# Two heads' attention scores issued together from the two halves of the TensorE array, in every second step of the attention loops

## What is computed

```python
# first block, one layer: heads of 64 columns (A: two maps of 32)
s = einsum('bqhmd,bkhmd->bhmqk', qa, ka_all) * 32 ** -0.5       # A: 4 heads, difference of two softmaxes
p = softmax(s);  a = p[:, :, 0] - lam * p[:, :, 1];  oa = einsum('bhqk,bkhd->bqhd', a, va_all)
s = einsum('bqhgd,bkhd->bhgqk', qb, kb_all) * 64 ** -0.5        # B: 6 heads, 2 key/value heads
s_nb, s_cx = ...                                                # C: 6 heads, neighbourhood with a bias, and context
# layer 0 also attends from the context tokens (to the context alone, 256 keys)

# second block, dilated attention: for each head and group g with (window, dilation)
scores = einsum(q_g, k_g) * 64 ** -0.5; scores = where(valid, scores, -inf)
o = sum_g alpha_g * softmax(scores_g) @ v_g                     # alpha from the groups' log-sums
```

## Time and profile before

| | |
|---|---|
| median of three runs | 1380.77 us (1374.21, 1380.77, 1384.84) |
| profiled execution, span from first to last instruction | 1381.9 us |
| mean granted TensorE clock | 0.954 of full |
| TensorE matmuls busy | 1213.9 us, 88% |
| TensorE weight loads busy | 958.0 us, 69% |
| VectorE busy | 756.3 us, 55% |
| ScalarE busy | 607.9 us, 44% |
| GpSimd busy | 253.1 us, 18% |
| DMA | 158.63 MB, 115 GB/s on the mean |

### The profile page before, as it was taken

How to read it: one execution, slowest core, us unless ns; L and a number is a source line. 1 busy time by engine, 2 the same in 40 slices (tenths; PEclk the granted TensorE clock), 3 DMA queues, 4 the chain that set the end, 5 groups by cost and what they waited for, 6 DMA issues and landing times.

```text
span 1381.9 us, 16760 instructions
## 1 busy us (share of the span) xinstructions
PE 1213.9 (88%) x5909; PEld 958.0 (69%) x5909; DVE 756.3 (55%) x1361; ACT 607.9 (44%) x1178; POOL 253.1 (18%) x323
## 2 busy tenths in 40 slices
PE   2678588889999797689999989898969999999997
PEld 2666356767666586567776768687858887888885
DVE  2746358478665264354445466665466555565533
ACT  2043244343665245345446454344344444444553
POOL 5108014024400312230230012100012211121100
PEclk9998789899999899889999999999989999999999
DMA  6518624333310322312220176454536665334301
GB/s 189 183 61 228 126 76 126 107 107 92 107 47 1 95 82 92 102 46 62 77 65 28 62 264 196 152 155 138 179 119 187 183 184 157 118 116 123 111 1 46
DMA packets 79475, 158.63 MB, mean 115 GB/s; under 512 B 5910, under 2 KB 6206, under 8 KB 79136
## 3 DMA queue, kind: packets, MB, share of 16 engines
q1 hardware_dynamic: 74992, 145.82, 34.5%
q0 software_dynamic: 4400, 11.73, 3.9%
HBM read 154.39 MB, written 3.78 MB: 114 GB/s over the span
## 4 chain that ended last, share of the span: by engine, by line
PE 69%; DVE 9%; ACT 8%; DMA 5%; POOL 4%; issue 4%; SPq 0%; ACTq 0%; POOLq 0%; DVEq 0%
PE bank L612 16%; PE bank L614 15%; PE bank L613 15%; PE bank L714 5%; PE bank L739 4%; DMA raw<-in_w_ada_dram 4%; PE bank L724 3%; PE bank L784 3%; PE bank L810 2%; DVE work L1486 2%; POOL small L1324 2%; DVE w_lo L1464 2%; ACT w_hi L906 2%; PE bank L795 2%; PE bank L632 1%
## 5 line engine op out<-in xcount | busy, mean ns | idle before, releaser
L612 PE MATMUL bank<-w_lo,h_hi 128*128 128x512 f32 (+1 forms) x1152 | 468.2, 406 | 48.5 <-DVE h_lo L1534 15.4
L614 PE MATMUL bank<-w_hi,h_hi 128*128 128x512 f32 (+1 forms) x1152 | 451.7, 392 | 0.0
L613 PE MATMUL bank<-w_hi,h_lo 128*128 128x512 f32 (+1 forms) x1152 | 451.5, 392 | 0.0
L1464 DVE TENSOR_TENSOR w_lo<-raw,w_hi 128x1024 fp32r<-128x1024 f32 x224 | 285.8, 1283 | 302.7 <-ACT w_hi L906 301.0
L906 ACT ACTIVATE w_hi<-raw 128x1024 fp32r<-128x1024 f32 x224 | 236.1, 1058 | 328.6 <-PE bank L614 268.8
L612 PEld LDWEIGHTS bank<-w_lo,h_hi 128*128 128x128 f32 x1152 | 225.9, 196 | 103.6 <-issue 32.7
L614 PEld LDWEIGHTS bank<-w_hi,h_hi 128*128 128x128 f32 x1152 | 224.5, 195 | 45.7
L613 PEld LDWEIGHTS bank<-w_hi,h_lo 128*128 128x128 f32 x1152 | 226.4, 197 | 41.0 <-issue 0.5
L1486 DVE SCALAR_TENSOR_TENSOR work<-raw,cvec,work 128x512 f32<-128x512 f32 x138 | 98.1, 764 | 34.2 <-DMA raw<-in_w_ada_dram 33.9
L714 PE MATMUL bank<-work 64*128 64x512 f32 (+3 forms) x240 | 99.6, 596 | 12.2 <-ACT stage L1082 12.2
L739 PE MATMUL bank<-work,stage 128*128 128x128 f32 x640 | 92.2, 286 | 1.8 <-ACT stage L1091 1.6
(11 more groups left out here) (161 smaller groups left out, 1167.0 us busy)
## 6 DMA issues: line engine op xcount, KB each, us to landing
raw<-in_b_w_in_dram SPq DMA_DIRECT2D x80, 512.0 KB, 3.7
raw<-in_w_in_dram SPq DMA_DIRECT2D x56, 512.0 KB, 3.8
raw<-in_w_ada_dram SPq DMA_DIRECT2D x48, 512.0 KB, 3.8
raw<-in_a_w_in_dram SPq DMA_DIRECT2D x48, 512.0 KB, 4.1
raw<-in_w_out_dram SPq DMA_DIRECT2D x16, 512.0 KB, 3.8
raw<-in_a_w_out_dram SPq DMA_DIRECT2D x16, 512.0 KB, 3.7
raw<-in_b_w_out_dram SPq DMA_DIRECT2D x8, 512.0 KB, 3.7
work<-bias POOLq DMA_DIRECT2D x24, 96.0 KB, 4.2
```

Source lines behind the costliest of these rows:

```text
L612: pe.matmul(bank, hT(h_hi, ph, kt, tt), w_lo[:, s, k, lo:lo + w], start=first, stop=False)
L613: pe.matmul(bank, hT(h_lo, ph, kt, tt), w_hi[:, s, k, lo:lo + w], start=False, stop=False)
L614: mm = pe.matmul(bank, hT(h_hi, ph, kt, tt), w_hi[:, s, k, lo:lo + w], start=False, stop=last)
L1464: dve.tensor_tensor(w_lo[:, i % SPLIT, :, :], raw[:, PIECE_AT[p] % RAW, :, :], w_hi[:, i % SPLIT, :, :].bitcast(F32), ALU.subtract).then_i ...
```

## The change

In every second step TensorE issues the scores of two units instead of one, and none in the other steps. The two units are heads in different halves of the array. For that B's heads are taken in the order 0, 3, 1, 4, 2, 5, and the dilated units in the order tile 0 of two heads, then tile 1 of the same two. A is scored one unit at a time as before. In the dilated attention the two units' matmuls alternate, group by group; its tile-1 units are paired only when four score banks are there. All other parts of a step keep their place, and go by the new order of units. The order of work on the other engines is changed by the order of units alone.

```diff
-    return [(layer, qt, kind, h) for kind, n in (("A", A_HEADS), ("B", B_HEADS), ("C", C_HEADS))
-            for qt in (ALL_TILES if layer == 0 else X_TILES) for h in range(n)]
+    return [(layer, qt, kind, h) for kind, order in (("A", range(A_HEADS)), ("B", (0, 3, 1, 4, 2, 5)), ("C", range(C_HEADS)))
+            for qt in (ALL_TILES if layer == 0 else X_TILES) for h in order]
+
+
+def scored_at(units, i):
+
+    if i + 1 >= len(units):
+        return ()
+    if units[i + 1][2] == "A":
+        return (i + 1,)
+    return (i + 1, i + 2) if i % 2 else ()
+
+
+def dil_unit(i):
+
+    return i % 4 // 2, i // 4 * 2 + i % 2
+
+
+def dil_scored_at(i, solo):
+
+    if i % 4 == 3:
+        return (i + 1, i + 2)
+    if i % 4 == 1:
+        return (i + 1, i + 2) if i > solo else (i + 1,)
+    return (i + 1,) if i % 4 == 2 and i - 1 <= solo else ()
...
-                    if i + 1 < len(units):
-                        score(units[i + 1], i)
+                    for n in scored_at(units, i):
+                        score(units[n], i)
...
-                units = [(qt, h) for h in range(DIL_HEADS) for qt in X_TILES]
+                units = [dil_unit(i) for i in range(2 * DIL_HEADS)]
...
-                def score(i):
-                    qt, h = units[i]
...
+                def score(*pair):
+                    for i in pair:
+                        qt, h = units[i]
...
+                        ring = SCORE_BANKS if i <= solo else SCORE_BANKS + (2, 3)
+                        for second in range(qt + 1):
+                            take(pe, ring[s_use[0] % len(ring)], "dscore", i, second)
+                            s_use[0] += 1
                     for g in range(DIL):
...
+                        for i in pair:
+                            qt, h = units[i]
+                            nk = (qt + 1) * P
+                            base = (h % 2) * HD
+                            at, second = dil_score_place(i, g)
+                            mm = pe.matmul(bank_of("dscore", i, second)[:, at:at + nk], dqkT[base:base + HD, g * 16 + h // 2, qt * P:(qt + 1) * P],
+                                           dqkT[base:base + HD, g * 16 + 8 + h // 2, 0:nk], start=True, stop=True)
+                            if g == DIL - 1:
+                                mm.then_inc(*scores.at(("dil", i)))
...
                     if i == 0:
-                        score(0)
-                    if i + 1 < len(units):
-                        score(i + 1)
+                        score(0, 1)
+                    elif i + 1 < len(units) and dil_scored_at(i, solo):
+                        score(*dil_scored_at(i, solo))
```

More of the change, by code:

```diff
@@ L440, in dil_score_place @@
         def dil_score_place(i, g):
-            nk = (i % 2 + 1) * P
+            nk = (dil_unit(i)[0] + 1) * P
             return (g * nk, 0) if nk == P or g < 2 else (0, 1)
@@ L766, in attention2 @@
                 solo = len(steps_beside("din"))
-                units = [(qt, h) for h in range(DIL_HEADS) for qt in X_TILES]
+                units = [dil_unit(i) for i in range(2 * DIL_HEADS)]
                 s_use = [0]
-                def score(i):
-                    qt, h = units[i]
[L772 to L778, removed]
-                    for g in range(DIL):
[L780 to L786, removed]
@@ new lines, in score @@
+                def score(*pair):
+                    for i in pair:
+                        qt, h = units[i]
+                        if h in (0, DIL_HEADS // 2) and qt == 0:
+                            for c in ([7, 6, 4, 3, 1, 0] if h == 0 else [18, 17, 15, 14, 12, 11]):
+                                for tt in X_TILES:
+                                    pe.wait_ge(*heads_turned.seen(("din", c, tt)))
+                        ring = SCORE_BANKS if i <= solo else SCORE_BANKS + (2, 3)
+                        for second in range(qt + 1):
+                            take(pe, ring[s_use[0] % len(ring)], "dscore", i, second)
+                            s_use[0] += 1
+                    for g in range(DIL):
+                        for i in pair:
[7 more added lines that the diff above has]
+                                mm.then_inc(*scores.at(("dil", i)))
@@ L788, in turn @@
                 def turn(i, part):
-                    n = DIL * (i % 2 + 1)
+                    n = DIL * (units[i][0] + 1)
                     lo = 4 * part
@@ L1227, in dil_exp @@
             def dil_exp(i):
-                n = DIL * P * (i % 2 + 1)
+                n = DIL * P * (dil_unit(i)[0] + 1)
                 act.wait_ge(*row_max.seen(("dil", i)))
@@ L1233, in dil_keep @@
             def dil_keep(i):
-                for part in range(i % 2 + 1):
+                qt = dil_unit(i)[0]
+                for part in range(qt + 1):
                     act.wait_ge(*probs_turned.seen(("dil", i, part)))
@@ L1237, in dil_keep @@
                         act.wait_ge(*attended.seen(("dil", i - 2)))
-                    lo, n = (512, 256) if part else (0, 512 if i % 2 else 384)
+                    lo, n = (512, 256) if part else (0, 512 if qt else 384)
                     act.activation(pT2[i % 2][:, lo:lo + n], bank_of("dpT", i, part)[:, 0:n], ACT.Copy).then_inc(*pT_a.at(("dil", i, part)))
@@ L1877, in dil_max @@
             def dil_max(i):
-                qt = i % 2
+                qt = dil_unit(i)[0]
                 nk = (qt + 1) * P
@@ L1903, in dil_step @@
                 if j >= 0:
-                    qt, h = j % 2, j // 2
+                    qt, h = dil_unit(j)
                     dve.wait_ge(*exps.seen(("dil", j)))
```

2 lines of the change are left out of this document (1 added, 1 removed).

## The result

| | before | after |
|---|---|---|
| median | 1381.03 us (4 runs, 1374.21 to 1384.84) | 1344.87 us (4 runs, 1344.82 to 1346.20) |
| ratio after / before | | 0.9749, 95% interval 0.9720 to 0.9778 |
| profiled execution, span | 1381.9 us | 1343.1 us |
| mean granted clock | 0.954 | 0.951 |

The forecast was 1341.4 us. The change gives 36.2 us by the medians and 38.8 by the profiled executions.

A forecast was written before the change was run, and what follows sets the result against it. TensorE, practically never idle in three stretches, was taken as the bound. Ceiling 46.9 us, less 3.2 (y turns), 1.5 (VectorE) and 2.8 (dilated turns), gives 39.4; 1380.8 - 39.4 = 1341.4 us, 8 in 10 for 1334 to 1356.

The forecast's parts named there:

- TensorE is full in the three stretches: Beside the layer-1 and dilated projections and in the dilated attention after: a microsecond off TensorE is one off the kernel.
- The second head is free: All paired scores, layers 0 and 1 and dilated: second head in another row group costs nothing, loads included; 45.7 us.
- half-overlap: Rival: 64-row passes follow program order, so B and C pairs save half; 16.6 us less, 1358; chance 0.08.
- narrow-load: Rival, dilated tile-0 pairs: twelve loads in a row, 1.45 us a group; 4.7 us less, 1346; inside the forecast's 0.72.
- y turns, 3.2: Layer 0 units 45, 47 and once in layer 1: bank-6 wait after y's turn loses its covering score; 3.2 us back.
- VectorE full, 1.5: Layer 0 steps 19 to 28, eight with w_ada sums: VectorE becomes the bound; 1.5 us back, between 0 and 2.3.
- Dilated turns, 2.8: Dilated attention alone, steps 16, 20, 24, 28: bank 6 twice running, TensorE waits for ScalarE's copy; 2.8 us back.
- The first dilated wait, 1.2: Very first dilated step: the 1.21 us idle wait for a bank goes, as two tile-0 units start in two banks.
- No other wait: Elsewhere in the odd-even rhythm cover is enough: nothing taken, up to 2 us in the range for 256-column stretches and attention ends.
- bank rival: Beside the projections pairs need both score banks one step earlier; eight B and C pairs lose 8.4 us; 1350; 0.13 with clock.
- The clock: Rival: new 1.7 us waits at y turns lower TensorE's clock, about 1.7 us each time; 1350; chance 0.13 shared with banks.

The follow-up runs named there:

- the kernel that gets rid of it: Changed kernel with layer 0's units 18, 19, 20 and 21 all scored one a step: 1343.69 us, ratio 0.9720 against the kernel before.

## Why the prediction was right

Forecast 1341.4, measured 1344.9, inside the range. The mechanism that carries the sum, two heads for the price of one, held. That the net came within 3.5 us is partly luck: terms that the sum had at nothing cost some 14 us, and some 10 that it hadn't counted came back, about half of them without a shown cause. The steps:

- *TensorE is full in the three stretches.* Held: a microsecond of score taken away there shortened the stage. Layer 1 beside its projection gained 5.9 for six pairs, 6.3 by the sum. ("Half the time or less" was misread for the other engines: by the earlier trace rows VectorE is at 55% beside the dilated projection, ScalarE at 54% behind it. It changed nothing.)
- *The second head is free,* 45.7 us. Held at both widths and for the loads: the spacings are 1.06, 0.63, 0.87 and 1.50, and the busy time is 46.9 us less. The half-overlap and narrow-load rivals are out; twelve narrow matmuls take 0.87 and not 1.45. The half-overlap rival came from counting the two passes of a product as two matmuls in program order. Counted as one, the two heads start (0 and 0.007 us) and end (1.123 and 1.129) in the order of the program, so these records don't speak against program order as such.
- *y turns, 3.2.* Three waits grew by 1.20, 1.05 and 1.06, 3.3 us. That the bank is the reason was only half right: with the banks exchanged half of the layer-0 growth stayed (0.80, 0.17 and 1.53 idle, against 1.86 and 1.77, and 0.66 and 0.72 before), and nearly all of layer 1's.
- *VectorE full, 1.5.* Its three waits are 0.42, 1.18 and 0.64, 2.2 us, against 0.94 before: 1.3.
- *Dilated turns, 2.8.* Four waits of 0.56 are 2.2, as said; the tail's wait, which was to stay, grew by 1.0. The last stretch gained 6.3.
- *The first dilated wait, 1.2.* Too small: the 3.4 us of half clock behind it went as well, 1.7. I had those rows and used them only against the change.
- *No other wait.* This step failed: "elsewhere in the odd-even rhythm the cover is enough" looked at even steps in the steady state, and the bank rival at pairs beside the projections. At the change of rings the pair comes upon ScalarE's backlog: 1.05 of overlap lost in each layer, and 2.42 more idle in layer 0, 1.4 more in layer 1, 5.9 in all. Beside the projections no pair waited, but three turns in even steps did, 1.6 us in all, for which the sum has nothing either.
- *The clock.* In layer 0 the half-clock time after unit 20 went from 3 to 12 us. Of that 6.8 us at 350.5 comes from the change, 3.4 us of time, shown by the kernel that gets rid of it; I had priced this at the y turns, where it didn't come. In layer 1 it is 3.4 us behind the wait, 1.7 of time, which stay away in the three kernels that score units 20 and 21 singly there. Over the whole run half-clock time is 127 us before and 132 after; the rest of the difference isn't tied to a cause.

39.4 forecast, less 5.9 (banks), 5.1 (clock), 1.6 (even steps beside the projections) and 1.0 (tail), plus 1.7 (clock kept at the first dilated step), 1.4 (the rest of the gain beside the dilated projection), 2.0 (half clock of before that was gone ahead of unit 20: 3.4 us in layer 0, 0.6 in layer 1) and 0.6 (turns and VectorE together a little cheaper) is 31.5. The six stretches show 34.2, the profiled executions 38.8 and the medians 36.2. Of the 2.7 us between sum and stretches, 1.1 and 1.3 are in the two with the split pair, and stay open. Of what lies above the stretches, 4.6 us, 5.7 are at the start, which no edit touched, and 2.1 in layer 1's type A, which had 17 us at half clock before and 10 after; others went the other way.

## What to carry to other kernels

Two products of 64 rows cost TensorE the time of one here if they stood next to each other in different halves of the array, so order the work that such neighbours come up; it pays only where TensorE is the full engine, and you see that in windows by stage. Then look at the steps that have lost their cover, and first where the rhythm changes (a new ring of banks, another engine's backlog): price a pair by its second buffer, which is needed one step earlier than before. When an experiment is to take a part of a change back, see that it takes back the waits too, and not only the order. A stage gain under 3 us can be read from the trace, stage by stage, but not from the time.

## What the runs showed of the hardware

- With two heads in different halves, 512 columns each, the four records start at 0, 0.007, 0.534 and 0.540 us in the kernel after. The first two carry no semaphore and the last two do, so I read them as both first passes and then both second passes. The second passes end 0.006 us apart.
- 64-row products in the same half run one after the other at 0.43 us a pass for 512 columns, and a group of them 0.19 us more (1.91 less four passes; 1.05 less two), whether it holds one head or two: that is what grouping alone saves.
- The clock fell to half in a stretch without any idle time of TensorE to speak of (0.33 of 3.50 us), after a step without a score and sixteen one-column matmuls; it did not with a score in each of the four steps. In layer 1, without such matmuls, it fell behind a wait of 2.42 us in seven kernels out of eight. Idle waits of 1.8 us at the y turns left it alone.
